# NSA loop: the product of reciprocal sums with the gates on GpSimd instead of VectorE

## What is computed

```python
o = gb[..., 0:1] * o_c + gb[..., 1:2] * o_s + gb[..., 2:3] * o_w
```

## Time and profile before

| | |
|---|---|
| median of 3 runs | 2984.41 us (2983.1 to 2986.3) |
| the profiled execution | 2985.21 us |
| its span in the profile | 2983.5 us |
| NSA loop, first scores to the output projection | 892.5 to 1065.2 us of the span |
| PE busy | 2871.4 us (96%) |
| DVE, ACT, POOL busy | 1380.9, 985.4, 473.5 us |

### The profile page before, as it was taken

One profiled execution on the slowest core, in us unless ns is written; L12 is line 12 of the kernel. 1 busy time (PEld: TensorE's weight loads), 2 busy tenths in 40 slices (PEclk: granted clock), 3 DMA queues, 4 the chain that ended last, 5 costly groups with the idle time before them and its releaser, 6 DMA issues. The chain is left out here.

```text
span 2983.5 us, 37773 instructions
## 1 busy us (share of the span) xinstructions
PE 2871.4 (96%) x14556; PEld 2362.4 (79%) x14556; DVE 1380.9 (46%) x1827; ACT 985.4 (33%) x1571; POOL 473.5 (16%) x363
## 2 busy tenths in 40 slices
PE   7999999997979999999999997999999999999998
PEld 5888888886866678888877775888888788888887
DVE  4464543334547755334355546353333456443333
ACT  4332432224234534222332223242223433332222
POOL 0021122100101222221012221112210012022210
PEclk9999999998979999999999998999999999999999
DMA  4323233334310012333332221233333332233331
GB/s 145 91 85 92 75 102 98 95 99 134 100 49 1 1 57 85 98 97 101 96 99 71 70 84 50 88 89 98 94 94 94 101 90 85 85 92 98 91 96 60
DMA packets 459669, 256.07 MB, mean 86 GB/s; under 512 B 9632, under 2 KB 447632, under 8 KB 459424
## 3 DMA queue, kind: packets, MB, share of 16 engines
q1 hardware_dynamic: 451328, 242.31, 27.8%
q10 hardware_dynamic: 7616, 9.97, 1.2%
q0 software_dynamic: 608, 2.16, 0.2%
HBM read 248.11 MB, written 2.10 MB: 84 GB/s over the span
## 5 line engine op out<-in xcount | busy, mean ns | idle before, releaser
L1430 DVE TENSOR_TENSOR w_lo<-w_raw,w_hi 128x1024 fp32r<-128x1024 f32 x461 | 625.8, 1359 | 951.4 <-ACT w_hi L1045 950.9
L466 PE MATMUL acc<-a_hi,w_hi 128*128 128x512 f32 x2264 | 892.4, 394 | 15.3 <-DVE w_lo L1430 8.5
L468 PE MATMUL acc<-a_hi,w_lo 128*128 128x512 f32 x2264 | 881.6, 389 | 0.0
L467 PE MATMUL acc<-a_lo,w_hi 128*128 128x512 f32 x2072 | 808.7, 390 | 0.0
L1045 ACT ACTIVATE w_hi<-w_raw 128x1024 fp32r<-128x1024 f32 x461 | 483.5, 1050 | 519.2 <-PE acc L468 459.6
L466 PEld LDWEIGHTS acc<-a_hi,w_hi 128*128 128x128 f32 x2264 | 427.2, 189 | 108.5 <-issue 13.1
L468 PEld LDWEIGHTS acc<-a_hi,w_lo 128*128 128x128 f32 x2264 | 426.8, 189 | 89.1
L467 PEld LDWEIGHTS acc<-a_lo,w_hi 128*128 128x128 f32 x2072 | 390.7, 189 | 80.1 <-issue 1.4
L468 PE MATMUL acc<-hid_hi,w_lo 128*128 128x512 f32 (+1 forms) x704 | 264.5, 376 | 0.0
L467 PE MATMUL acc<-hid_lo,w_hi 128*128 128x512 f32 (+1 forms) x704 | 264.5, 376 | 0.0
L466 PE MATMUL acc<-hid_hi,w_hi 128*128 128x512 f32 (+1 forms) x704 | 264.5, 376 | 0.0
(11 more groups left out here) (302 smaller groups left out, 3485.4 us busy)
## 6 DMA issues: line engine op xcount, KB each, us to landing
w_raw<-ffn_w_gate SPq DMA_DIRECT2D x88, 512.0 KB, 3.8
w_raw<-ffn_w_up SPq DMA_DIRECT2D x88, 512.0 KB, 3.8
w_raw<-gm_w_in SPq DMA_DIRECT2D x64, 512.0 KB, 4.1
w_raw<-ffn_w_down SPq DMA_DIRECT2D x64, 512.0 KB, 3.7
w_raw<-ret_w_in SPq DMA_DIRECT2D x48, 512.0 KB, 3.7
w_raw<-gm_w_out SPq DMA_DIRECT2D x32, 512.0 KB, 3.8
w_raw<-ffn_w_down SPq DMA_DIRECT2D x32, 384.0 KB, 3.3
w_raw<-nsa_w_in SPq DMA_DIRECT2D x21, 512.0 KB, 3.8
```

The costliest lines, as they stand in the source:

```text
L466: pe.matmul(o_bank, lhs_hi, rhs_hi, start=start, stop=False)
L467: pe.matmul(o_bank, lhs_hi, rhs_lo, start=False, stop=False)
L468: return pe.matmul(o_bank, lhs_lo, rhs_hi, start=False, stop=stop)
L1430: dve.tensor_tensor(w_lo[:, slot, :, :], w_raw[:, slot, :, :], w_hi[:, slot, :, :].bitcast(f32), ALU.subtract).then_inc(lo_done, 1)
```

## The change

The reciprocal stays on VectorE and signals a new semaphore, `scl_done`. The product is written into GpSimd's program, ahead of the sum of the branches of the same group; it waits for `scl_done` and for the PE transposes of the previous `SS`, and signals `rs_inv`, for which PE waits as before. VectorE's wait for these transposes becomes a wait for the product of two groups earlier, whose `scl` buffer it overwrites. The order of PE's instructions is unchanged.

```diff
@@ VectorE, NSA loop @@
                         dve.wait_ge(exp_done, exps_through(v))
-                        wait(dve, spread_mm, g)
-                        link(dve.reciprocal(scl[:, g % 2, :], rs[:, g % 2, :]))
-                        dve.tensor_tensor(SS[:, :].rearrange("p (c x d) -> p c x d", c=CH, x=2),
-                                          scl[:, g % 2, :].rearrange("p (c x) -> p c x", x=2).unsqueeze(3).broadcast_to(over),
-                                          gates.unsqueeze(3).broadcast_to(over), ALU.mult).then_inc(rs_inv, 1)
+                        wait(dve, rs_inv, g - 1)
+                        dve.reciprocal(scl[:, g % 2, :], rs[:, g % 2, :]).then_inc(scl_done, 1)
@@ GpSimd, NSA loop @@
                     for g in range(H_NSA):
                         hp = g % (H_NSA // 2)
 
+                        gate0 = NSA_GATE0 + 1 + g // (H_NSA // 2) + 6 * hp
+                        over = [P, CH, 2, HD]
+                        if g == 0:
+                            pool.wait_ge(nv_done, 1)
+                        pool.wait_ge(scl_done, g + 1)
+                        wait(pool, spread_mm, g)
+                        pool.tensor_tensor(SS[:, :].rearrange("p (c x d) -> p c x d", c=CH, x=2),
+                                           scl[:, g % 2, :].rearrange("p (c x) -> p c x", x=2).unsqueeze(3).broadcast_to(over),
+                                           gt[:, :, gate0:gate0 + 4:3].unsqueeze(3).broadcast_to(over), ALU.mult).then_inc(rs_inv, 1)
+
                         pool.wait_ge(ocmp_done, CH)
                         pool.wait_ge(o_rd, g + 1)
```

More of the change, by code:

```diff
@@ L320, in build @@
             sc_even sc_odd sm_done pexp pc_done pc_tr pc_t pvc_mm ocmp_done dve_step
-            s_mm max_done exp_done t_mm pt_done pv_mm rs_inv spread_mm spread_done o_rd o_add o_hi_done o_lo_done
+            s_mm max_done exp_done t_mm pt_done pv_mm rs_inv scl_done spread_mm spread_done o_rd o_add o_hi_done o_lo_done
             y_tr y_sb stored""".split()
@@ L336, in build @@
          sc_even, sc_odd, sm_done, pexp, pc_done, pc_tr, pc_t, pvc_mm, ocmp_done, dve_step,
-         s_mm, max_done, exp_done, t_mm, pt_done, pv_mm, rs_inv, spread_mm, spread_done, o_rd, o_add, o_hi_done, o_lo_done,
+         s_mm, max_done, exp_done, t_mm, pt_done, pv_mm, rs_inv, scl_done, spread_mm, spread_done, o_rd, o_add, o_hi_done, o_lo_done,
          y_tr, y_sb, stored) = [s[n] for n in names]
@@ L1698, in attention @@
                     if 0 <= v < n and STEPS[v][2] == last_part:
-                        br, hp, _ = STEPS[v]
                         g = v // len(PARTS)
-                        gates = gt[:, :, NSA_GATE0 + 1 + br + 6 * hp:NSA_GATE0 + 1 + br + 6 * hp + 4:3]
-                        over = [P, CH, 2, HD]
                         dve.wait_ge(exp_done, exps_through(v))
-                        wait(dve, spread_mm, g)
-                        link(dve.reciprocal(scl[:, g % 2, :], rs[:, g % 2, :]))
-                        dve.tensor_tensor(SS[:, :].rearrange("p (c x d) -> p c x d", c=CH, x=2),
-                                          scl[:, g % 2, :].rearrange("p (c x) -> p c x", x=2).unsqueeze(3).broadcast_to(over),
-                                          gates.unsqueeze(3).broadcast_to(over), ALU.mult).then_inc(rs_inv, 1)
+                        wait(dve, rs_inv, g - 1)
+                        dve.reciprocal(scl[:, g % 2, :], rs[:, g % 2, :]).then_inc(scl_done, 1)
                     if 0 <= v < n:
```

## The result

The changed kernel takes 2991.72 us (median of 15 runs, 2988.49 to 2993.19) against 2984.7 us for the kernel before (15 runs as well): a ratio of 1.0022, 95% interval 1.0014 to 1.003, or 7.0 us more. The profiled execution has 2991.39 us and a span of 2989.7 us, 6.2 us more than before. The forecast was 3002 us, its range began at 2993. The sign was right, the size was two and a half times too large.

The account below looks back on a forecast made before the run. The prediction took PE to bound the kernel, through a closed cycle containing the product. Later products (6.2 + 4.4 + 0.4 = 11.0 us) plus clock falls (6.4) gave 17.4 us more, forecast 3002 us, range 2993 to 3011.

Parts of the forecast that it names:

- The cycle: NSA loop: PE's transposes L928 lie on a closed cycle through maxima, reciprocal and product; a product 0.72 us later lengthens the group 0.72.
- The freed copy on DVE: DVE without the product: the copy to `pt` could start near 915.4 instead of 916.00, worth nothing, as DVE idles 0.62 us.
- The reciprocal's new wait: DVE's reciprocal, waiting for the product of two groups earlier: the wait was met some 10 us before.
- The product on POOL: Groups 0 to 8: POOL's product takes 1.28 us, so L928 starts 0.69 us later in each, 6.2 us in all.
- Behind `o_lo`: Groups 9 to 14: the product queues on POOL after `o_lo`, L928 starts 0.73 us later in each, 4.4 us in all.
- The last group: Last group of the loop: the product ends at 1063.54, L928 starts at 1063.59 instead of 1063.18, 0.4 us later.
- The clock: Groups 9 to 14: PE holes of 1.46 us bring four falls to 1.2 GHz at 1.6 us each, 6.4 us.
- rival B: NSA loop: later products cost 11.0 us but the clock does not fall, 2995.4 us; chance 0.27.
- Contention: POOL's product beside DVE's copy from PSUM: neither is lengthened, cost zero.

Follow-up runs that it names:

- the reciprocal first: Changed kernel with o_lo behind the next group's product and VectorE's reciprocal issued ahead of the step's maxima: 2978.37 us against 2984.49, ratio 0.9978.
- the kernel with the copy late: Changed kernel, VectorE's copy to `pt` after a group's last part made to wait for GpSimd's product: 2994.09 us against 2983.84, ratio 1.0031.
- the doubled product: Changed kernel, the same product made once more by GpSimd into an unused tile ahead of the real one: 3025.19 us against 2983.84, ratio 1.0139.

## Why the prediction was wrong, step by step

**The cycle: right.** That L928 lies on a closed cycle and that nothing absorbs a later product was read off the two branches of the kernel before. Every run kept it: 0.40 us later in the first branch gave 10.12 to 10.52, 0.72 us earlier in the second gave 10.84 to 10.12, 1.11 us later gave 11.63.

**The freed copy on DVE: right, in this order.** It was worth nothing, even when delayed by 1.8 us. The sentence that relieving DVE pays only where DVE ends a wait of PE held too, but which waits DVE ends depends on its order: with the reciprocal first, the same 0.69 us on DVE held PE up in every group and cost 0.5 us (10.53 against 10.04). The reciprocal's new wait was misread: the product of two groups earlier had ended some 19 us before, not 10, which costs nothing either way.

**The product on POOL: a term mis-sized, and the first cause of the miss.** I took 1.28 us from a sum of two different tiles and had said that no row showed spread operands; it took 1.04. POOL took it up 0.08 us after the reciprocal and not 0.14, PE followed after 0.06 us, as the rows had it, and not 0.05. Reciprocal to L928 became 1.37 us instead of 1.66, so the slip was 0.40 us and not 0.69: nine groups, 3.6 us and not 6.2.

**Behind `o_lo`: mechanism right, size off by the same term.** The product started as `o_lo` ended (within 0.04 us) and took 1.04: 0.46 us a group instead of 0.73, for six groups 2.7 us and not 4.4. That the lost collision is made up for by the queue held: 0.72 us gone, 0.78 come.

**The last group: predicted 0.4 us later, came out 0.3 us earlier,** because the fall of the clock that the kernel before had there did not happen in the profiled execution. With a fall at this place, as in the kernel with the copy late, it was 1.3 us later than before.

**The clock: the second cause, and the larger error.** I counted four falls in groups 9 to 14, 6.4 us; there was none. One part follows from the product: the hole was 1.19 us and not 1.46. But the step itself was weak, a hole of 1.34 us before one fall taken as a mark above which falls come: in two of the ten traces the clock stayed up after that very hole, and after the 1.89 us of the last group it stayed up in seven. At 1.53 to 1.60 us two of nine holes were followed by a fall, at 2.31 us all seven. By these an estimate for six holes of 1.46 us is one or two falls and not four; no run had holes of that size, and what besides the length of the hole decides was not settled. The Trainium skill's warning cited for rival B (TensorE: Matmul & The Clock Gate, "Why this matters for your kernels": idle gaps of about twice 1.46 us) is too lenient as well: holes of 1.53 us already cost two falls, and the measurement decides.

**Contention: right.** POOL's product and DVE's copy ran beside each other at 1.04 and 1.22 us.

**The range.** Rival B named what happened, a slip without falls, and gave 2995.4 where 2991.72 was measured. Its own uncertainty was the product, for which I had written 0.69 to 2.26 us as bounds, yet the range's lower end used 1.13. With the measured slips the direct part is 9 x 0.40 + 6 x 0.46 = 6.4 us, thus 2991: the unknown form of the instruction deserved the room that I gave to the clock.

## What to carry to other kernels

Where a loop has two halves that differ in one start time, read their difference before anything else: it is a measurement of what a delay costs. An operation that goes to another engine's queue pays for what is queued ahead of it there as well as for its own length; here the queue cost 0.78 us and the slower engine 0.40. And ask for the order before the engine: moving 0.2 us of reciprocal ahead of 1.2 us of maxima took away the hole that the slower product had made in the old order, and moving one unrelated instruction (`o_lo`) behind the product gained 3.8 us without any change of engine.

## What the runs showed of the hardware

- A GpSimd tensor-tensor instruction on 128x512 float32 took 1.27 us with two different full tiles, 1.04 to 1.06 with one or two spread operands, and 1.04 as a product of one tile with itself. A sum took the same as a product in the two forms tried as both (two full tiles, two spread operands).
- A VectorE product of two SBUF operands took 1.41 us when a GpSimd instruction had started 0.4 us before it and 0.69 us when not, while a VectorE copy or maximum from PSUM was not lengthened beside GpSimd.
- After holes of 1.53 to 1.60 us in an otherwise busy loop TensorE's granted clock fell to 0.50 for 3.4 us in two of nine groups, at a price of 1.6 us each; after 2.31 us it fell in all seven. After 1.19 us it didn't in groups 9 to 14 of three traces.
- The same hole was not always followed by a fall: at the loop's start (1.33 to 1.34 us) the clock fell in eight of ten traces, in the last group (1.89 us, in some kernels with one of 1.19 us behind it) in two of the nine without the doubled product.
